# Local and global attention heads in alternation, and the last steps of the key search in the next iteration

## The reference, cut to what matters

```python
proj = h @ w_in[l]                      # queries, keys, values, latents, indexer
# A (local): window of 128 tokens in chunks of 64, with sinks
logits = einsum(qc, kb) * HEAD_DIM ** -0.5 - slopes * dist
out_a = softmax_with_sink(logits) @ vb
# B (global): each query keeps the 256 keys with the best indexer score
dots = relu(einsum('bqhd,bsd->bqhs', qib, k_idx))
score = where(visible, einsum('bqh,bqhs->bqs', wb, dots), -inf)
_, idx = lax.top_k(score, 256)
out_b = softmax(q @ kg.T * HEAD_DIM ** -0.5 - slopes * dist) @ vg
mix = concatenate([out_a, out_b]) @ w_o[l]
```

## Time and profile before

| | |
|---|---|
| median of 3 runs | 3391.96 us (3391.65 to 3392.4) |
| the profiled execution | 3388.4 us, its span 3386.6 us |
| PE busy | 2987.1 us, 88% of the span |
| PE weight loads busy | 2439.3 us, 72% |
| DVE busy | 1701.3 us, 50% |
| ACT busy | 1574.6 us, 46% |
| POOL busy | 318.4 us, 9% |

### The profile page before, as it was taken

One profiled execution on the slowest core, in us unless ns is written; L12 is line 12 of the kernel. 1 busy time (PEld: TensorE's weight loads), 2 busy tenths in 40 slices (PEclk: granted clock), 3 DMA queues, 4 the chain that ended last, 5 costly groups with the idle time before them and its releaser, 6 DMA issues. The chain is left out here.

```text
span 3386.6 us, 42835 instructions
## 1 busy us (share of the span) xinstructions
PE 2987.1 (88%) x14649; PEld 2439.3 (72%) x14649; DVE 1701.3 (50%) x3080; ACT 1574.6 (46%) x3023; POOL 318.4 (9%) x990
## 2 busy tenths in 40 slices
PE   5689888888878878778899699999999999999997
PEld 2467676666766666667788588788878887888876
DVE  2146677676776677765355344244432444244422
ACT  1357787767677577685433222232222322232222
POOL 0012222212121121020011000000000000000000
PEclk8688889888888888788899799999999999999999
DMA  5011110000000000000355433343323433343323
GB/s 208 15 45 38 47 32 29 23 26 26 16 14 26 22 8 9 4 5 4 122 170 155 130 99 93 118 138 98 99 87 123 143 93 99 111 143 99 94 92 106
DMA packets 316075, 254.86 MB, mean 75 GB/s; under 512 B 9153, under 2 KB 271905, under 8 KB 315809
## 3 DMA queue, kind: packets, MB, share of 16 engines
q1 hardware_dynamic: 282544, 236.29, 22.5%
q10 hardware_dynamic: 33392, 16.81, 1.7%
HBM read 219.50 MB, written 33.57 MB: 75 GB/s over the span
## 5 line engine op out<-in xcount | busy, mean ns | idle before, releaser
L1961 ACT ACTIVATE p_hi<-raw 128x1024 fp32r<-128x1024 f32 x264 | 279.3, 1058 | 693.8 <-PE dbank L1932 354.7
L2035 DVE TENSOR_TENSOR p_lo<-raw,p_hi 128x1024 fp32r<-128x1024 f32 x264 | 323.4, 1225 | 425.5 <-ACT p_hi L1961 425.4
L1115 ACT ACTIVATE logit<-tbank 128x512 f32<-128x512 f32 (+3 forms) x448 | 214.6, 488 | 288.5 <-PE tbank L851 286.5
L867 PE MATMUL obank<-vb,logit 128*128 128x64 f32 x2176 | 318.1, 294 | 0.0
L1289 DVE TENSOR_SCALAR_CACHE_REDUCE above<-score,cand 128x384 uint8<-128x384 f32 (+6 forms) x224 | 315.9, 1410 | 4.4
L1137 ACT ACTIVATE signs<-score,pick 128x512 int8<-128x512 f32 (+6 forms) x224 | 304.3, 1359 | 21.9 <-POOL pick L633 13.4
L867 PEld LDWEIGHTS obank<-vb,logit 128*128 128x128 f32 x2176 | 312.5, 219 | 0.0
L836 PE MATMUL lbank<-kb,qb_hi 128*128 128x512 f32 (+3 forms) x320 | 166.8, 521 | 156.5 <-DVE mx L1348 134.2
L1913 PE MATMUL gbank<-x_hi,p_hi 128*128 128x512 f32 x704 | 275.1, 391 | 29.3 <-DVE p_lo L2035 29.3
L1930 PE MATMUL dbank<-p_hi,a_hi 128*128 128x512 f32 x704 | 278.5, 396 | 17.0 <-DVE a_lo L2063 14.0
L851 PE MATMUL tbank<-ident,logit 128*128 128x128 f32 x1336 | 256.5, 307 | 36.6 <-ACT logit L1105 19.3
(11 more groups left out here) (219 smaller groups left out, 5280.5 us busy)
## 6 DMA issues: line engine op xcount, KB each, us to landing
raw<-in_w_gate_up SPq DMA_DIRECT2D x176, 512.0 KB, 3.8
raw<-in_w_down SPq DMA_DIRECT2D x88, 512.0 KB, 3.7
ada<-in_w_ada ACTq DMA_DIRECT2D x32, 512.0 KB, 3.8
wada<-in_w_ada SPq DMA_DIRECT2D x4, 2048.0 KB, 15.5
x_in<-in_x SPq DMA_DIRECT2D x16, 512.0 KB, 4.0
mixT<-oT SPq DMA_DIRECT2D x32, 256.0 KB, 2.3
mix<-mixT SPq DMA_DIRECT2D x16, 512.0 KB, 6.3
x_rows<-in_x SPq DMA_DIRECT2D x16, 512.0 KB, 4.6
```

The lines of the kernel that those rows point to most:

```text
L867: mm = nc.tensor.matmul(obank[o % 2][:, h * HD:(h + 1) * HD], logit[:, i % 4, (4 * g + j) * P:(4 * g + j + 1) * P], v, start=(g == 0 and j ...
L1961: nc.scalar.activation(p_hi[:, s], raw[:, s], ACT.Copy).then_inc(panel_high, 1)
L2035: nc.vector.tensor_tensor(p_lo[:, s], raw[:, s], p_hi[:, s].bitcast(F32), ALU.subtract).then_inc(panel_ready, 1)
```

## The change

Iterations 0 to 13 take the heads in one order of 16 slots, `BOTH_KINDS`: A0 A1 A2 B0 A3 B1 A4 B2 A5 B3 A6 B4 A7 B5 B6 B7 (A of block b + 2, B of block b). The chunks of scores stand before slot 0 and after slots 0, 1 and 2; the global queries of block b come before slot 0; the steps for block b + 3 come after slots 3 (transposes), 4 to 8 (projection), 9 (gains), 10 (latent), 12 (latent_up) and 13 (local queries), and the norm of block b + 4 after slot 11. The `mod` steps move: 12 in the prologue (2 before), 4 in iterations 0 to 3, 16 in iterations 13 and 14, one after each global head; before, there were two per iteration among the local heads and a third in iterations 0 to 3, until all 32 were used up in iteration 12.

The closing steps are three for even b and four for odd b, since the pass that writes `bias_b` is now one of its own (`mask_bias`). For b up to 13 the last two (ties part 1, and the bias) are done in slots 0 and 1 of iteration b, and part 0 in slot 15 of iteration b - 1. The parts of the ties now take `between`, so a head's own work goes between their operations, except behind the running sum. The weights of both searches are new. POOL's last step of the modulation and the turning of its columns move into block 15's global heads.

```diff
--- before.py
+++ after.py
@@ -177,39 +177,49 @@
...
-SEARCH = [("bit", j) for j in range(32)] + [("ties", 0), ("ties", 1)]
+SEARCH = [("bit", j) for j in range(32)] + [("ties", 0), ("ties", 1), ("bias", 0)]
 
 ON_SCALAR = [("bit", j) for j in range(32)]
-AFTER_SCALAR = [("above", 0), ("ties", 0), ("ties", 1)]
+AFTER_SCALAR = [("above", 0), ("ties", 0), ("ties", 1), ("bias", 0)]
 
 
 def searched_by_scalar(b):
     return b % 2 == 1
 
 
-def vector_weight(b, slot):
-
-    it, kind, h = slot
-    scoring = it + 2 < NB and h <= 3
-    if kind == "A":
-        return (0.0 if it == b - 2 else 1.0) if scoring else 4.0
-    room = 0.5 + 0.41 * (it + 1)
-    if it + 3 < NB and h in (2, 4, 6):
-        room -= 1.0
-    if it == b - 2 and b > 2:
-        room -= {5: 2.0, 6: 100.0, 7: 100.0}.get(h, 0.0)
-    return max(room, 0.0)
-
-
-def scalar_weight(b, slot):
-
-    it, kind, h = slot
-    if kind == "A":
-        return 0.0 if it == b - 2 and h <= 3 else 1.8
-    room = 0.5 + 0.3 * (it + 1)
+BOTH_KINDS = [("A", 0), ("A", 1), ("A", 2), ("B", 0), ("A", 3), ("B", 1), ("A", 4), ("B", 2),
+              ("A", 5), ("B", 3), ("A", 6), ("B", 4), ("A", 7), ("B", 5), ("B", 6), ("B", 7)]
+
+
+def slots_of(it):
+
+    return BOTH_KINDS if it + 2 < NB else [("B", h) for h in range(HEADS)]
+
+
+SCORED = 3
+
+
+def vector_weight(b, it, at, kind):
+
+    both = it + 2 < NB
+    if both and at < SCORED:
+        if it == b - 2:
+            return 0.0
+        return 3.5 if at == 2 or b < 4 else 0.0
+    if both and it == b - 2 and at == 15 and b > 3:
+        return 0.0
+    return 2.5 if kind == "A" else 0.5 + 0.3 * (it + 1)
+
+
+def scalar_weight(b, it, at, kind):
+
+    both = it + 2 < NB
+    if both and at < SCORED and it == b - 2:
+        return 0.0
+    room = 1.8 if kind == "A" else 0.5 + 0.25 * (it + 1)
     if it + 3 < NB:
-        room -= {1: 2.5, 3: 2.5, 4: 1.0, 5: 2.5}.get(h, 0.0)
-    return max(room, 0.3)
+        room -= {1: 2.5, 8: 1.5, 11: 3.0, 13: 2.5, 14: 2.5}.get(at, 0.0)
+    return max(room, 0.2)
 
 
 def spread(weights, n):
@@ -224,24 +234,22 @@
 
 def search_slots(b):
 
-    slots = []
-    for it in (b - 2, b - 1):
-        if it + 2 < NB:
-            slots += [(it, "A", h) for h in range(HEADS)]
-        slots += [(it, "B", h) for h in range(HEADS)]
+    slots = [(it, at, kind, h) for it in (b - 2, b - 1) for at, (kind, h) in enumerate(slots_of(it))]
+    after = [(b, at, kind, h) for at, (kind, h) in enumerate(slots_of(b))][0:2] if b + 2 < NB else []
     vector, scalar = {}, {}
-    if searched_by_scalar(b):
-        wts = [scalar_weight(b, slot) for slot in slots[:-3]]
-        for slot, r in zip(slots, spread(wts, len(ON_SCALAR))):
-            scalar[slot] = [(b, ON_SCALAR[n]) for n in r]
-        for slot, action in zip(slots[-3:], AFTER_SCALAR):
-            vector[slot] = [(b, action)]
+    actions = AFTER_SCALAR if searched_by_scalar(b) else SEARCH[-3:]
+    if after:
+        closing = slots[-(len(actions) - 2):] + after
     else:
-        wts = [vector_weight(b, slot) for slot in slots[:-2]]
-        for slot, r in zip(slots, spread(wts, len(SEARCH) - 2)):
-            vector[slot] = [(b, SEARCH[n]) for n in r]
-        for slot, action in zip(slots[-2:], SEARCH[-2:]):
-            vector[slot] = [(b, action)]
+        closing = slots[-(len(actions) - 1):] + slots[-1:]
+    bits = slots[0:slots.index(closing[0])]
+    weight, per_slot, which = ((scalar_weight, scalar, ON_SCALAR) if searched_by_scalar(b) else
+                               (vector_weight, vector, SEARCH[:-3]))
+    wts = [weight(b, it, at, kind) for it, at, kind, h in bits]
+    for (it, at, kind, h), r in zip(bits, spread(wts, len(which))):
+        per_slot[it, kind, h] = [(b, which[n]) for n in r]
+    for (it, at, kind, h), action in zip(closing, actions):
+        vector.setdefault((it, kind, h), []).append((b, action))
     return vector, scalar
 
 
@@ -292,7 +300,7 @@
         for h in range(HEADS):
             steps.append(("head", "A", b, h, (), ()))
             front_a(b + 1, h)
-            if b and h in (1, 7):
+            if h in (0, 1, 2, 4, 6, 7):
                 modulate()
         steps += [("queries", "A", b + 1), ("gains", b + 1), ("latent", b + 1), ("latent_up", b + 1),
                   ("norm", b + 2)]
@@ -302,28 +310,24 @@
             steps.append(("scores", nxt, 0))
         else:
             steps.append(("queries", "B", b))
-        for h in range(HEADS if nxt else 0):
-            at = (b, "A", h)
-            steps.append(("head", "A", nxt, h, tuple(vector.get(at, ())), tuple(scalar.get(at, ()))))
+        if nxt:
+            add(("queries", "B", b))
+        for at, (kind, h) in enumerate(slots_of(b)):
+            slot = (b, kind, h)
+            steps.append(("head", kind, nxt if kind == "A" else b, h, tuple(vector.get(slot, ())),
+                          tuple(scalar.get(slot, ()))))
+            if nxt and at + 1 < len(key_chunks("B", nxt)):
+                add(("scores", nxt, at + 1))
             if b + 3 < NB:
-                front_a(b + 3, h)
-            if h + 1 < len(key_chunks("B", nxt)):
-                add(("scores", nxt, h + 1))
-            if h == 2:
-                add(("queries", "B", b))
-            if h in (1, 7):
+                n = b + 3
+                add(*{3: [("transposes", n)], 4: [("proj", n, 0)], 5: [("proj", n, 1)], 6: [("proj", n, 2)],
+                      7: [("proj", n, 3)], 8: [("proj", n, 4)], 9: [("gains", n)], 10: [("latent", n)],
+                      12: [("latent_up", n)], 13: [("queries", "A", n)]}.get(at, []))
+            if b + 4 < NB and at == 11:
+                add(("norm", b + 4))
+            if kind == "B" and ((h == 3 and b < 4) or b in (NB - 3, NB - 2)):
                 modulate()
-        for h in range(HEADS):
-            at = (b, "B", h)
-            steps.append(("head", "B", b, h, tuple(vector.get(at, ())), tuple(scalar.get(at, ()))))
-            if b + 3 < NB:
-                add(*{0: [("queries", "A", b + 3), ("gains", b + 3)], 2: [("latent", b + 3)],
-                      4: [("latent_up", b + 3)]}.get(h, []))
-            if b + 4 < NB and h == 4:
-                add(("norm", b + 4))
-            if h == 5 and b < 4:
-                modulate()
-            if b == NB - 2 and h == 1:
+            if b == NB - 1 and h == 0:
                 add(("mod_rows",))
     return steps, beside
 
@@ -671,7 +675,7 @@
                     for b, action in s[5] + tuple(x for x in s[4] if x[1][0] == "above"):
                         move_pick(b, action)
                     shift()
-                if s[0:4] == ("head", "B", NB - 1, 0):
+                if s[0:4] == ("head", "B", NB - 1, 4):
                     modulate()
                 if s[0] not in ("norm", "gains"):
                     continue
@@ -818,7 +822,9 @@
                 g = h // (HEADS // A_KV)
                 if c == 0 and h == 0:
 
-                    last = ("latent_up", b) if kind == "A" else ("queries", "B", b)
+                    last = ("queries", kind, b)
+                    if kind == "A":
+                        last = max(last, ("latent_up", b), key=plan.split0.get)
                     pe.wait_ge(split_done, plan.split0[last] + SPLITS[last[0]])
                 o, n = key_chunks(kind, b)[c]
                 m = plan.chunk0[i] + c
@@ -1269,9 +1275,10 @@
                     threshold_bit(b, action[1], between)
                 elif action[0] == "above":
                     count_next(b, between)
+                elif action[0] == "ties":
+                    ties(b, action[1], between)
                 else:
-                    ties(b, action[1])
-                    between(3)
+                    mask_bias(b)
 
             def count_next(b, between):
 
@@ -1296,7 +1303,7 @@
                 link(nc.vector.scalar_tensor_tensor(cand[:], cand[:], following, reject[:],
                                                     ALU.bitwise_xor, ALU.bitwise_xor), between)
 
-            def ties(b, part):
+            def ties(b, part, between):
 
                 L = P * (b + 1)
                 thr = (pick if searched_by_scalar(b) else cand)[:].bitcast(F32)
@@ -1309,23 +1316,29 @@
                     else:
                         dve.wait_ge(lat_ssq, NB)
                     nc.vector.tensor_scalar(equal[:, 0:L], score[:, b % 2, 0:L], thr, None, ALU.is_equal)
+                    between(1)
 
                     link(nc.vector.tensor_scalar(above[:, 0:L], score[:, b % 2, 0:L], thr, None,
-                                                 ALU.is_lt, ALU.add, accum_out=count[:]))
+                                                 ALU.is_lt, ALU.add, accum_out=count[:]), between, 2)
                     link(nc.vector.tensor_tensor_scan(rank[:, 0:L], equal[:, 0:L], equal[:, 0:L], 0.0,
                                                       ALU.add, ALU.max))
 
```

(19 more changed lines are left out.)

## The result

The changed kernel takes 3451.48 us (median of 4 runs, 3450.52 to 3455.0) against 3391.81 before (4 runs): a ratio of 1.0183, with a 95% interval of 1.0167 to 1.0199. It is 60 us slower where 80 us faster were forecast. Its profiled execution took 3455.0 us, with a span of 3453.2.

What follows compares the result with a forecast made beforehand. Local heads were taken as limited by PE, global heads by DVE and ACT passes. Terms 35 - 88 - 22 - 10 + 5 = -80 us gave 3308 from the profiled execution, 3312 against the median; range 3240 to 3400.

Steps and rivals of the forecast that it cites:

- Prologue, +35: Blocks 0 and 1: ten added modulation steps, with load waits and PE time, cost 35 us (bounds +17 to +45).
- Iterations 4 to 12, -88: Alternating local and global heads, with 18 modulation steps removed, saves 88 us there (bounds +15 to -150).
- Carried to 929.6 us: Scales iteration 10's gain of 12 us by 7.48 to all of iterations 4 to 12, less 2: -88.
- The sum for iteration 10: Slots 0 to 2, 3 to 8 and 9 to 15 take 24 + 37 + 51 = 112 us against 124.2.
- The stop at gains stays ... +4: Slots 9 to 15: DVE still waits at gains for POOL's root, +4 us, half of 7.1.
- The 24 us of slots 0 to 2: Iteration 10's first slots: 30.3 us falls to 24 without modulation step and transposes; added DVE work of 5.4 us hidden.
- Iterations 0 to 3, -22: Eight modulation steps leave, -15 us, and alternation wins 7: -22 (bounds -35 and 0).
- Rival 2: Whole kernel: alternation brings nothing, only modulation steps move; -8 us, 3384 us; chance 0.10.
- The early closing steps: Slots 0 to 2: ties part 1 and the bias, 5.4 us of DVE, are hidden beside its 8.5 in 30.3.
- Rival 3: Front block late: part 0, low parts and gains wait cost 15.1 us an iteration, 3448 us; chance 0.18 with lesser forms.
- Rival 1: Iterations 4 to 12: steadier PE work brings the higher clock back, -150 us there, 3250 us in all; chance 0.20.
- The weight loads as the measure: Slots 3 to 8: if weight loads mark PE's limit, the stretch takes about 31 us, not 37; sum -125.

Runs made afterwards that it cites:

- e12: The kernel before, with no sign pass of the odd searches in global head 0: 3354.15 us, ratio 0.9905.
- e1: The kernel before, with only the 32 modulation steps moved to where the changed kernel has them: 3401.09 us, ratio 1.0047.
- e11: The changed kernel with one line alone, no sign pass of the odd searches in slot 9: 3403.34 us, ratio 1.0056.
- e2: The changed kernel, but ACT copies the global queries at once instead of one head later: 3437.81 us, ratio 1.0144.
- e4: The changed kernel, but the closing steps end in slot 15 of iteration b - 1, none in the next iteration: 3484.35 us, ratio 1.0282.
- e6: The kernel before, with ties interleaved with head work, last two closing steps in the next iteration's local heads 0 and 1, transposes later: 3325.80 us, ratio 0.9823.
- e9: The changed kernel with queries copied at once, no sign pass in slot 9, DVE's bits weighted towards slots 4 to 8: 3355.11 us, ratio 0.9909.
- e5: e2 with DVE's search bits weighted towards slots 4 to 8 and away from other slots: 3385.78 us, ratio 0.9997.
- e13: e6 without sign passes in global head 0 and with the changed kernel's modulation steps, e9's old-order counterpart: 3316.34 us, ratio 0.9793.

## Why the prediction was wrong, point by point

- *Prologue, +35*: +39, by the mechanism and the waits forecast. Right.
- *Iterations 4 to 12, -88*: -4. The first step that failed is "Carried to 929.6 us". The estimate for iteration 10 was 12 us of gain and 9.8 were measured, but the other eight had less or a loss. Iteration 10 was a special case: in the kernel before it alone had three sign passes ahead of the gains root, a wait of 7.1 us where the other eight had 2.4 to 4.6. And a ratio of times scales a price that is the same in each iteration as if it grew with b. Why the even iterations stood out before (124.2 against 104.8 and 121.2) stays open: with the waits at `gains` gone (e12) they still do, 116.7 against 105.1 and 113.7.
- *The sum for iteration 10 was right by luck.* Of the 88 us the prediction gave 33 to the modulation steps that leave and 55 to the order. By e1 the steps alone give iteration 10 its whole gain (124.2 to 113.9), and the order gives +0.5. So the step that failed in the mechanism is that DVE's passes, once spread, run at a share of 0.95 and PE's work in slots 9 to 15 takes 35 us: measured were 0.84 and 42.75, with many short stops in place of the few long ones and a clock of 0.72.
- *"The stop at gains stays ... +4"*: 4.3 us in iteration 10, as said, but only there is this less than before; in each of the other eight it is more, in all 48.8 us instead of 33.1. The term was mis-sized: taking its cause away is worth 48 us over the changed kernel (e11), with PE's echo and the clock in it, and 32 over the kernel before (e12).
- *The 24 us of slots 0 to 2*: 26.6 in iteration 10. That the global queries, moved ahead of slot 0, hold one of two work banks until ACT has done a head was not seen; it is 43.8 us of wait, worth 14 by e2. The list of steps was read for its instructions, not for the banks that they hold.
- *Iterations 0 to 3, -22*: +26, outside its bounds. The modulation steps' new places give +12 (e1), where the forecast had -15 for them, and the order +13, where it had -7.
- *Iterations 13 and 14, -5*: +5, within the bounds.
- *Modulation steps at 1.84 us*: 3.1 each in iterations 4 to 12. Rival 2's sum for them alone gave -8; e1's median is 14 above the kernel before. Iterations 0 to 3 were 27 us worse than that sum had them, 4 to 12 22 better, the prologue 4 and iterations 13 and 14 8 worse.
- *The early closing steps*, costed as hidden and no more, are the best part of the change: 33 us (e4), or 61 with the ties' interleaving in the old order (e6).
- *Rival 3*, which gave 3448, came close to the number by the wrong sum. Its half at `gains` is true (e11). Its other half is not: no wait of PE for the local queries' low parts shows in iterations 4 to 12, and undoing the closing steps cost time. Its 7.1 us at `gains` for each iteration were 5.4 in the mean. It had no term for the bank.
- *Rival 1*: the clock did not come back in the changed kernel (0.85), although PE's gaps of over 4 us in iterations 4 to 12 fell from 16 (86.6 us) to 6 (28.9 us): shorter ones took their place. In e9, with 36 us fewer of stops, it is 0.91, and PE's time for the same instructions is 692 us instead of 740. The product of 0.47 us before a stop and 0.79 behind it agrees with the rule of the Trainium skill (TensorE: Matmul & The Clock Gate, HAM oscillation) cited in the prediction; the price of a stop can therefore be more than its length.
- *The weight loads as the measure* (the Trainium skill, Trainium Kernel Development and Optimization, Reading a trace): in slots 3 to 8 of iteration 10 PE was busy for 32.9 of 33.6 us and its weight loads for 24.4, and the stretch took 33.6, between the 37 and the 31. But e5, which put more of DVE's work into slots 4 to 8 and left PE's alone, brought 52 us. No run here decides what limited those slots; that DVE had room in them does not depend on it.

What stays open: e9 against e13 shows that the alternating order with its planner loses 39 us with the repairs made, and where the waits are, but not whether better weights for ACT's passes would close it. Nor do the parts add up to the 51 us between e1 and the changed kernel: the repairs overlap (e9), and one of them, at `gains`, helps the old order too (e12).

## What to carry to other kernels

Before a gain in one iteration is multiplied, compare that iteration with its neighbours: a price that it alone has, or that doesn't grow with the size of the iteration, must be taken out and counted by itself. And when one part of a change can be run alone, as e1, read the rest against that run and not against the kernel before: a single iteration may come out as forecast for another reason. When a step moves, look for what it holds (a bank until another engine has done a head) and for what stands ahead of its inputs on every in-order queue, the small ones too: here two sign passes ahead of one small operation on POOL cost 48 us in the new order and 32 in the old. A change of several parts is best priced part by part, since its best part (the closing steps with the ties' interleaving, 61 us) may be hidden by the others.

## What was not expected of the hardware

The same PE instructions of iterations 4 to 12, in the same order, take 740 us at a granted clock of 0.85 (the changed kernel) and 692 at 0.91 (e9), where only passes and copies of other engines were placed otherwise. Cutting long stops into short ones did not bring the clock back (0.85 before and after). Each modulation step, 16 products of one column, takes 1.84 us at the higher level (clock 1.00 from 178.6 to 180.4 in the kernel before) and 3.5 at the lower (0.50 from 149.5 to 153.0), though it streams almost nothing: a step with hardly a moving column follows the clock as well.
